# Weight requests, index products and the last tile's normalised rows between a hybrid block's mixer and its experts

## Chip, cores and metric

The kernel runs on one core of a Trainium2 chip. Its time is device microseconds (us) from start to end of the program on that core; a profiled execution also has a span, from the first to the last instruction of its trace. Five engines work side by side and wait for each other by semaphores: TensorE (PE; PEld is its weight load), VectorE (DVE), ScalarE (ACT), GpSimd (POOL) and SyncE (SP), which here issues nearly all DMA transfers from one queue.

## Reference

One decoder layer on 1024 tokens of 1024 channels, in float32. A mixer (a state space scan beside causal attention) is projected back to 1024 channels and added to the residual x. Then comes the part that matters here, a mixture of 32 experts in 4 groups:

```python
h = rms_norm(x, pre_norm_ffn) * (1.0 + sc2) + sh2
g_prob = softmax(h @ w_group_router + b_group)        # one group of 4
e_sel  = expert logits (8) of the chosen group
e_w, e_idx = top_k(softmax(e_sel), 2)                 # two experts of 8
hid = silu(h @ w_gate[e]) * (h @ w_up[e])             # 1024 -> 256
out = sum over the two experts of weight * (hid @ w_down[e])   # 256 -> 1024
x = x + g2 * rms_norm(out, post_norm_ffn)
```

Each expert has 3 MiB of weights: gate, up and down, 1 MiB each.

## The kernel before

The rows (tokens) are cut into NT = 8 tiles of P = 128. The trace of interest begins in the second half of the program, a loop over t from -3 to 7 that is written out for each engine. In step t the scan of tile t + 2 or t + 3, the output projection of tile t + 1 (`project`, L1523) and the routing of tile t (`h2_T_of` L1535, `route` L1542, `logits_of` L2004, `choose` L2007 to L2027) are interleaved by hand. For tile t the residual sum is `x2` (`x2_of`, L1981), the normalised row is `h2` = x2 * rstd * A2 + B2 (`h2_of` L1987 and `shifted` L1992, both on VectorE). SP stores both to DRAM (`x2_rows`, `h2_rows`) and loads the residual input of tile t + 2 (`load_x`, L1276). The profile prints names without buffer numbers, and so `x2` as `x`, `h2` as `h`.

*Slots.* Every token goes to two experts. Each expert's tokens are cut into halves of 64, and two halves, of the same expert or of neighbours, make one step of the expert stage (23 steps here). For that, the index stage counts tokens per expert (`both`, `before`: sums over a tile and over the tiles ahead; rank products with `tri_lt` and `ones`, L1590 and L1601 to L1604), gives each token a lane in its half (`own_rank`, `own_lane`, `lanes`) and a half (`half_j`), and turns these into a list of rows by matmuls of one-hot tables: `lane_v` (lane one-hot times token number, made by ScalarE at L1789 for tiles 0 to 6; `lane_last`, made by VectorE at L2053, for tile 7) against `half_oh` (L2138), at L1612. The lane table is written twice side by side, so that the 128 output rows hold the 64 lanes twice. Small VectorE instructions that need each other's results are chained by `link`, which waits for the one just issued. `busy(bank, n)` is n matmuls of `ident` by `ones` whose result nobody reads; they stand where TensorE would idle.

*Experts.* A gather on GpSimd (L1240) fetches the 128 rows of a step from `h2_rows`, TensorE turns them (L1621), multiplies by gate and up (L1645), turns the hidden layer, multiplies by down (L1671). The second half's weights are first copied to a common place by ScalarE and VectorE (`nearer`: L1826 and L2211). VectorE's L2205 evicts the result and so marks the end of a step. Weights live in a ring of RING = 6 slots that overlay buffers of earlier stages: slot 4 lies on the output projection's weights, slot 5 on `zs`, `h2`, the small scan tables and the router's weights. SP asks for the parts of experts 0 to 5 at hand-picked places, and from expert 6 on in the loop

```python
for e in range(RING, E):
    landed(e - 2)                      # all three parts of expert e-2
    used = last_step(e - RING)         # last step that reads expert e-6
    sp.wait_ge(S["gate_done"], used)
    load_gate(sp, e, r)
    sp.wait_ge(S["gu_done"], used)
    load_up(sp, e, r)
    sp.wait_ge(S["dn_done"], used)
    load_down(sp, e, r)
```

SP works through its list in order, so a wait holds back all that stands behind it, row stores as well.

## Time and profile before

| | |
|---|---|
| median of 3 runs | 1017.91 us (1013.28 to 1018.14) |
| profiled execution | 1020.63 us, of which its span is 1018.6 us |
| mean granted TensorE clock | 0.980 of full |
| TensorE busy | 963.5 us (95%) |
| VectorE busy | 514.3 us (50%) |
| ScalarE busy | 306.0 us (30%) |
| GpSimd busy | 215.5 us (21%) |
| moved by DMA | 192.56 MB, mean 189 GB/s |

All times of rows are microseconds from the span's start. The granted clock is a share of 2.4 GHz and has two levels, 1.00 and 0.50 (1.2 GHz); a mean between them is a stretch with both. A matmul in float32 appears as two passes, so counts of matmuls in rows are twice those in the code, except for transposes, which are one pass. The expert stage runs from about 690 to 973 us, the sums over the two experts and the output behind it to the end.

### The profile page before, as it was taken

How to read it: one execution, taken by the hardware profiler on the slowest of the kernel's cores; microseconds unless marked ns; L12 is line 12 of the kernel's file. 1: busy time of each engine (PE TensorE's matmuls, PEld its weight loads, DVE VectorE, ACT ScalarE, POOL GpSimd, SP SyncE). 2: the span in 40 equal slices, each digit the busy share in tenths (PEclk: the TensorE clock that was granted, in tenths of full speed). 3: DMA queues.
4: the chain of work that ended last, by engine and by line, in shares of the span. 5: the costliest groups of instructions: out<-in, count | busy, mean ns of one | idle time of the engine just before them, and what ended most of it. 6: DMA issues, size and time to landing. Idle time of an engine off the chain costs nothing.

```text
span 1018.6 us, 15260 instructions
## 1 busy us (share of the span) xinstructions
PE 963.5 (95%) x5501; PEld 578.7 (57%) x5501; DVE 514.3 (50%) x935; ACT 306.0 (30%) x598; POOL 215.5 (21%) x267
## 2 busy tenths in 40 slices
PE   8999999999989999989999999999999998999946
PEld 6544444444456556559666665695555554555512
DVE  2366456444765555556577775573333332333327
ACT  3220001223453434432232222133333332333313
POOL 2200001221600840003344322012222211222003
PEclk9999999999999999999999999999999998999968
DMA  9996523000000000005021121889999999999557
GB/s 323 359 357 227 190 82 52 0 1 0 7 1 1 1 2 1 1 1 208 1 83 62 63 83 62 350 317 361 420 416 407 398 396 391 418 405 407 201 218 289
DMA packets 54929, 192.56 MB, mean 189 GB/s; under 512 B 15354, under 2 KB 26690, under 8 KB 39362
## 3 DMA queue, kind: packets, MB, share of 16 engines
q1 hardware_dynamic: 46500, 173.10, 44.1%
q0 software_dynamic: 7056, 18.36, 4.7%
q8 instruction: 48, 0.79, 0.3%
q10 hardware_dynamic: 1296, 0.07, 0.1%
q14 instruction: 29, 0.24, 0.1%
HBM read 174.21 MB, written 24.64 MB: 195 GB/s over the span
## 4 chain that ended last, share of the span: by engine, by line
PE 36%; DMA 13%; DVE 2%; issue 1%; SPq 1%; ACT 1%; ACTq 0%; POOL 0%; POOLq 0%; DVEq 0%
PE PS L1523 11%; DMA ring<-in_w_down_dram 11%; PE PS L1645 8%; PE PS L1671 4%; PE PS L1437 1%; PE PS L1447 1%; PE PS L1701 1%; PE PS L1542 1%; PE PS L1491 1%; DMA ring<-in_w_gate_dram 1%; PE PS L1621 1%; PE PS L1535 1%; PE PS L1506 1%; DMA y_g<-y_rows 1%; DVE y_sum L2256 1%
## 5 line engine op out<-in xcount | busy, mean ns | idle before, releaser
L1645 PE MATMUL PS<-ring,xg_T 128*64 x736 | 165.5, 384 | 5.5 <-ACT near_gu L1826 4.5
L1645 PE MATMUL PS<-near_gu,xg_T 128*64 128x256 f32 x736 | 165.5, 384 | 0.0
L1645 PEld LDWEIGHTS PS<-ring,xg_T 128*64 128x64 f32 x736 | 101.8, 139 | 66.8 <-issue 21.0
L1523 PE MATMUL PS<-w_out_sb,cat_T 128*128 128x512 f32 x256 | 118.0, 603 | 1.4 <-DVE y_sc L1975 1.0
L1011 PE MATMUL PS<-hT,w_x 128*128 128x512 f32 x256 | 112.0, 594 | 0.0
L1645 PEld LDWEIGHTS PS<-near_gu,xg_T 128*64 128x64 f32 x736 | 101.8, 139 | 0.0
L434 POOL TENSOR_SCALAR rstd<-stat 128x1 f32<-128x1 f32 (+1 forms) x48 | 21.8, 453 | 372.4 <-ACT junk L614 181.3
L1671 PE MATMUL PS<-ring,hid_T 128*64 x184 | 83.8, 598 | 0.4 <-DVE hid_T L2198 0.4
L1671 PE MATMUL PS<-near_dn,hid_T 128*64 128x512 f32 x184 | 83.9, 598 | 0.0
L1011 PEld LDWEIGHTS PS<-hT,w_x 128*128 128x128 f32 x256 | 47.8, 190 | 58.1 <-issue 57.8
L915 DVE TENSOR_REDUCE row_max<-PS 128x1 f32<-128x1024 f32 (+7 forms) x64 | 48.2, 753 | 60.8 <-PE PS L1164 60.6
L2189 DVE TENSOR_TENSOR hid<-PS,hid_s 128x128 f32<-128x128 f32 x46 | 11.2, 286 | 129.2 <-PE PS L1645 129.2
L1162 PE MATMUL PS<-kT,qT 96*128 96x512 f32 (+4 forms) x192 | 74.9, 500 | 1.1 <-ACT qT L645 1.1
L661 ACT ACTIVATE probs<-PS,row_max 128x1024 f32<-128x1024 f32 (+7 forms) x64 | 47.4, 740 | 94.7 <-DVE row_max L915 94.3
L1523 PEld LDWEIGHTS PS<-w_out_sb,cat_T 128*128 128x128 f32 x256 | 47.0, 193 | 47.6 <-issue 47.3
L1240 POOL DMA_INDIRECT x_g<-h_rows,idx_i x23 | 39.8, 1729 | 152.3 <-PE PS L1621 135.3
L1060 PE MATMUL PS<-w_z,hT 128*128 128x512 f32 x128 | 56.2, 592 | 0.0
L1174 PE MATMUL PS<-ident,probs 128*128 128x128 f32 x288 | 43.4, 278 | 12.8 <-ACT probsT L669 6.6
L1174 PEld LDWEIGHTS PS<-ident,probs 128*128 128x128 f32 x288 | 30.9, 141 | 30.1 <-ACT probs L661 24.8
L1671 PEld LDWEIGHTS PS<-ring,hid_T 128*64 128x64 f32 x184 | 23.3, 136 | 42.6 <-issue 41.4
L1826 ACT ACTIVATE near_gu<-ring 128x2048 f32 x23 | 43.8, 1906 | 11.4 <-SPq L1306 7.8
L1069 PE MATMUL PS<-w_rest,hT 128*128 128x424 f32 x128 | 46.9, 519 | 0.0
(333 smaller groups left out, 1562.1 us busy)
## 6 DMA issues: line engine op xcount, KB each, us to landing
ring<-in_w_gate_dram SPq DMA_DIRECT2D x32, 1024.0 KB, 11.4
ring<-in_w_up_dram SPq DMA_DIRECT2D x32, 1024.0 KB, 13.4
ring<-in_w_down_dram SPq DMA_DIRECT2D x32, 1024.0 KB, 16.2
ada_later<-in_ada_w_dram SPq DMA_DIRECT2D x16, 1024.0 KB, 4.8
ada_first<-in_ada_w_dram SPq DMA_DIRECT2D x16, 512.0 KB, 9.6
y_g<-y_rows SPq DMA_DIRECT2D x8, 1024.0 KB, 11.9
x_in<-in_x_dram SPq DMA_DIRECT2D x8, 512.0 KB, 7.8
w_out_sb<-in_w_out_dram SPq DMA_DIRECT2D x1, 4096.0 KB, 13.1
```

Source lines behind the costliest of these rows:

```text
L661: act.activation(probs[b][:, 0:n], PS[:, 2 * b:2 * b + 2, :].rearrange("p a n -> p (a n)")[:, 0:n], ACT.Exp, bias=row_max[:, b:b + 1], acc ...
L915: dve.tensor_reduce(row_max[:, b:b + 1], PS[:, 2 * b:2 * b + 2, :].rearrange("p a n -> p (a n)")[:, 0:n], AX_X, ALU.max, negate=True).then ...
L1011: last = pe.matmul(BANK[4 + n % 4][:, :], w_x[:, k, ct * P:(ct + 1) * P], hT[:, k, hh * HALF:(hh + 1) * HALF], start=(k == 0), stop=(k == ...
L1060: last = pe.matmul(BANK[t % 2][:, 0:IN_SSD], hT[:, k, t * P:(t + 1) * P], w_z[:, k, :], start=(k == 0), stop=(k == KC - 1))
L1069: last = pe.matmul(BANK[6 + t % 2][:, 0:REST], hT[:, k, t * P:(t + 1) * P], w_rest[:, k, :], start=(k == 0), stop=(k == KC - 1))
L1162: pe.matmul(BANK[2 * b + c0 // HALF][:, 0:c1 - c0], qT[h][0:depth(h), i * P:(i + 1) * P], kT[h][0:depth(h), c0:c1], start=True, stop=c1 < ...
L1174: last = pe.transpose(BANK[4 + j // 4][:, j % 4 * P:(j % 4 + 1) * P], probs[g % 2][:, j * P:(j + 1) * P], ident[:, :])
L1240: pool.indirect_dma_start(x_g[n % 2][:, :], None, h2_rows, bass.IndirectOffsetOnAxis(ap=idx_i[:, n:n + 1], axis=0), bounds_check=T - 1, oo ...
L1523: last = pe.matmul(BANK[out_bank(t) + j], cat_T[t % 2][:, k, :], w_out_sb[:, k, j * HALF:(j + 1) * HALF], start=(k == 0), stop=(k == KC - 1))
L1645: last = pe.matmul(BANK[2 + s_][rows_, 0:FF], xg_T[b][:, k, rows_], gu[u][:, s_, k, :], start=(k == 0), stop=(k == KC - 1))
L1671: last = pe.matmul(BANK[5 + j][rows_, :], hid_T[b][:, k, rows_], (near_dn[k] if u else far[:, k, :])[:, j * HALF:(j + 1) * HALF], start=(k ...
L1826: act.activation(near_gu[:, 0, :], w[:, 0 * KC * FF:1 * KC * FF], ACT.Copy).then_inc(S["near_gu_act"], 1)
```

## The change

Weight requests are moved ahead on SP: expert 2, up and down of expert 3 and gate and up of expert 1 behind step t = 4 of the row loop; expert 0 and down of expert 1 in step 5; gate 3, expert 4 and gate 5 behind step 6; down 5 in step 7; up 5 stays behind the first gathers. Each stands behind waits for the last reader of what its space held. `lane_v` moves to a place that no slot uses.

The lane tables are written once, 64 wide, the index products give 64 rows, and VectorE reads them twice with a shift of partitions. For tile 7 alone, `h2` is made in another way: VectorE forms x2 * A2 and a diagonal matrix of rstd, TensorE adds the product of these to B2 in PSUM, and ScalarE copies the sum out. On VectorE the second lane comparison moves behind `choose`, and two chains of small instructions are interleaved, with waits (`after`) on marked ones. TensorE has fewer dummy matmuls; the rank products that need no result of tile 7 come first, and the counts get a semaphore of their own. `x2T_half` and a wait inside `route` split the router's transposes and products in halves, for each tile.

```diff
...
 lane_oh = place("lane_oh", R_S + 16384, [P, 2, NT, LANE])
-lane_v = place("lane_v", R_A + 137216, [P, 2, NT - 1, 2, LANE])
-lane_last = place("lane_last", R_A + 86016, [P, 2, 2, LANE])
+lane_v = place("lane_v", R_A + 24576, [P, 2, NT - 1, LANE])
+lane_last = place("lane_last", R_A + 86016, [P, 2, LANE])
+h2_diag = place("h2_diag", R_A + 86016 + 2 * LANE * 4, [P, P])
...
             if t == NT - 1:
-                sp.wait_ge(S["catT_done"], NT)
-                sp.wait_ge(S["yo_done"], NT - 1)
-                load_gate(sp, 3, 3)
+                sp.wait_ge(S["lg_done"], NT)
+                load_down(sp, 5, 5)
+            if t == NT - 3:
+                sp.wait_ge(S["ssd_y"], NT)
+                load_expert(sp, 0, 0)
+                sp.wait_ge(S["cat_done"], NT)
+                load_down(sp, 1, 1)
...
                 load_x(t + 2)
-            if t == NT - 3:
-                sp.wait_ge(S["ssd_y"], NT)
-                load_expert(sp, 0, 0)
-                sp.wait_ge(S["cat_done"], NT)
-                load_expert(sp, 1, 1)
+            if t == NT - 4:
+                sp.wait_ge(S["ssd_off"], NT - 1)
+                sp.wait_ge(S["ssd_m"], 2 * NT)
+                sp.wait_ge(S["cat_done"], 5)
                 load_expert(sp, 2, 2)
-        load_up(sp, 3, 3)
-        load_down(sp, 3, 3)
-        sp.wait_ge(S["yo_done"], NT)
-        load_gate(sp, 4, 4)
+                load_up(sp, 3, 3)
+                load_down(sp, 3, 3)
+                load_gate_up(sp, 1, 1)
+            if t == NT - 2:
+                sp.wait_ge(S["catT_done"], NT)
+                sp.wait_ge(S["yo_done"], NT - 1)
+                load_gate(sp, 3, 3)
+                sp.wait_ge(S["yo_done"], NT)
+                load_expert(sp, 4, 4)
+                sp.wait_ge(S["h2_stored0"], 16 * NT // 2)
+                load_gate(sp, 5, 5)
...
             return sp.value_load(free_i[0:1, e:e + 1], min_val=1, max_val=NTILE)
-        for e in range(RING - 3):
+        for e in range(RING - 2):
             landed(e)
-        sp.wait_ge(S["lg_done"], NT)
+        sp.wait_ge(S["h2_stored1"], 16 * NT // 2)
...
         sp.wait_ge(S["xg_loaded1"], 16)
-        load_up(sp, 4, 4)
-        load_down(sp, 4, 4)
-        load_expert(sp, 5, 5)
-        landed(RING - 3)
+        load_up(sp, 5, 5)
...
                 last = pe.transpose(BANK[4 + k // 4][:, k % 4 * P:(k % 4 + 1) * P], x2[t % 2][:, k::KC], ident[:, :])
+                if k == KC // 2 - 1:
+                    last.then_inc(S["x2T_half"], 1)
...
             pe.wait_ge(S["h2T_act"], t + 1)
-            pe.wait_ge(S["h2T_dve"], t + 1)
             for k in range(KC):
+                if k == KC // 2:
+                    pe.wait_ge(S["h2T_dve"], t + 1)
...
         pe.wait_ge(S["y_out"], NT - 1)
-        busy(7, 18)
+        for j in range(D // HALF):
+            pe.matmul(BANK[6 + j], ident[:, :], B2[:, j * HALF:(j + 1) * HALF], start=True, stop=False)
+        busy(3, 2)
         h2_T_of(NT - 1)
-        busy(7, 4)
         route(NT - 1)
-        busy(7, 16)
+        pe.wait_ge(S["h2_scaled"], 1)
+        for j in range(D // HALF):
+            last = pe.matmul(BANK[6 + j], h2_diag[:, :], y_sc[:, j * HALF:(j + 1) * HALF], start=False, stop=True)
+        last.then_inc(S["h2_sum"], 1)
+        busy(5, 2)
+        for b in (2, 3):
+            pe.matmul(BANK[b][:, 0:E], ones[:, :], before[:, NT - 1, :], start=True, stop=False)
         pe.wait_ge(S["rt_both"], NT)
-        pe.matmul(BANK[2][:, 0:E], ones[:, :], before[:, NT - 1, :], start=True, stop=False)
-        pe.matmul(BANK[2][:, 0:E], ones[:, :], both[:, NT - 1, :], start=False, stop=True)
-        pe.matmul(BANK[3][:, 0:E], tri_lt[:, :], both[:, NT - 1, :], start=True, stop=False)
-        pe.matmul(BANK[3][:, 0:E], ones[:, :], before[:, NT - 1, :], start=False, stop=True).then_inc(S["ranks_done"], 1)
-        busy(5, 22)
+        pe.matmul(BANK[2][:, 0:E], ones[:, :], both[:, NT - 1, :], start=False, stop=True).then_inc(S["counts_done"], 1)
+        pe.matmul(BANK[3][:, 0:E], tri_lt[:, :], both[:, NT - 1, :], start=False, stop=True).then_inc(S["ranks_done"], 1)
+        busy(5, 14)
+        pe.wait_ge(S["h2_done"], NT)
...
             for t in range(t0, t1):
-                rows_v = lane_last[:, j, :, :] if t == NT - 1 else lane_v[:, j, t, :, :]
-                last = pe.matmul(BANK[6][:, 0:2 * NTILE], rows_v.rearrange("p u n -> p (u n)"), half_oh[:, j, t, :],
+                last = pe.matmul(BANK[6][0:LANE, 0:2 * NTILE], lane_last[:, j, :] if t == NT - 1 else lane_v[:, j, t, :], half_oh[:, j, t, :],
...
         last.then_inc(S["idx_done"], 1)
-        busy(5, 26)
+        busy(5, 24)
...
         def h2T_half(t):
-            act.wait_ge(S["h2T_done"], t + 1)
+            act.wait_ge(S["x2T_half"], t + 1)
...
             for t in range(NT - 1):
-                last = act.activation(lane_v[:, j, t, :, :], lane_oh[:, j, t:t + 1, :].to_broadcast([P, 2, LANE]), ACT.Copy, scale=v_tab[:, j, t:t + 1])
+                last = act.activation(lane_v[:, j, t, :], lane_oh[:, j, t, :], ACT.Copy, scale=v_tab[:, j, t:t + 1])
             last.then_inc(S["lanes_scaled"], 1)
+            if j == 0:
+                act.wait_ge(S["h2_sum"], 1)
+                act.wait_ge(S["h2_stored1"], 16 * (NT // 2 - 1))
+                act.activation(h2[1][:, :], PS[:, 6:8, :].rearrange("p a n -> p (a n)"), ACT.Copy).then_inc(S["h2_done"], 1)
...
             for j in range(2):
-                ins = dve.tensor_scalar(lane_last[:, j, :, :], iota_row[:, 0:LANE].unsqueeze(1).to_broadcast([P, 2, LANE]),
-                                        lane[:, j, t:t + 1], v_tab[:, j, t:t + 1], ALU.is_equal, ALU.mult)
-            link(ins)
+                dve.tensor_scalar(lane_last[:, j, :], iota_row[:, 0:LANE], lane[:, j, t:t + 1], v_tab[:, j, t:t + 1], ALU.is_equal, ALU.mult)
...
                 h2T_half(t)
-                lanes(1)
...
                 choose(t)
-        h2_of(NT - 1)
+        def mark(ins):
+            step_dve[0] += 1
+            ins.then_inc(S["dve_step"], 1)
+            return step_dve[0]
+        def after(n):
+            dve.wait_ge(S["dve_step"], n)
+        dve.wait_ge(S["x2_done"], NT)
+        dve.tensor_tensor(y_sc[:, :], x2[(NT - 1) % 2][:, :], A2[:, :], ALU.mult)
+        dve.wait_ge(S["rstd_x2"], NT)
+        dve.tensor_scalar(h2_diag[:, :], ident[:, :], rstd[:, 6, NT - 1:NT], None, ALU.mult).then_inc(S["h2_scaled"], 1)
...
         wide = lambda v, n: v[:, :].unsqueeze(2).to_broadcast([P, NT, n])
-        shifted(NT - 1)
+        flat2 = lambda v: v[:, :, :].rearrange("p j t -> p (j t)")
+        lanes(1)
         dve.wait_ge(S["x2_stored0"], 16 * NT // 2)
-        dve.memset(near32, -FAR)
+        far_row = mark(dve.memset(near32, -FAR))
+        dve.wait_ge(S["counts_done"], 1)
+        halves = mark(dve.tensor_scalar(n_half, BANK[2][:, 0:E], 1.0, 1.0 / HT, ALU.max, ALU.mult))
         dve.wait_ge(S["ranks_done"], 1)
-        link(dve.tensor_scalar(n_half, BANK[2][:, 0:E], 1.0, 1.0 / HT, ALU.max, ALU.mult))
-        link(dve.tensor_scalar(n_half, n_half, 0.49, FAR, ALU.add, ALU.add))
-        link(dve.tensor_tensor_scan(incl, n_half, near32, 0.0, ALU.add, ALU.add))
-        link(dve.tensor_tensor(base_t, incl, n_half, ALU.subtract))
-        own_rank(NT - 1, NT, 3)
-        own_lane(NT - 1, NT)
+        for j in range(2):
+            hits = mark(dve.tensor_tensor(prod[:, j, NT - 1, :], picked[:, j, NT - 1, :], BANK[3][:, 0:E], ALU.mult))
+        after(halves)
+        whole = mark(dve.tensor_scalar(n_half, n_half, 0.49, FAR, ALU.add, ALU.add))
+        after(hits)
+        r, hi, lo = (v[:, :, NT - 1] for v in (rank, high, lane))
+        own = mark(dve.tensor_reduce(r, prod[:, :, NT - 1, :], AX_X, ALU.add))
+        after(whole)
+        summed_up = mark(dve.tensor_tensor_scan(incl, n_half, near32, 0.0, ALU.add, ALU.add))
+        after(own)
+        upper = mark(dve.tensor_scalar(hi, r, HT / 2 - 0.5, FAR * HT, ALU.subtract, ALU.add))
+        after(summed_up)
+        based = mark(dve.tensor_tensor(base_t, incl, n_half, ALU.subtract))
+        after(upper)
+        lower = mark(dve.scalar_tensor_tensor(lo, hi, FAR * HT, r, ALU.subtract, ALU.subtract, reverse1=True))
+        after(based)
+        of_base = mark(dve.tensor_tensor(prod[:, :, :, :].rearrange("p j t e -> p (j t) e"), picked[:, :, :, :].rearrange("p j t e -> p (j t) e"),
+                                         base_t.unsqueeze(1).to_broadcast([P, 2 * NT, E]), ALU.mult))
+        after(lower)
         last_lanes(NT - 1)
-        flat2 = lambda v: v[:, :, :].rearrange("p j t -> p (j t)")
-        link(dve.tensor_tensor(prod[:, :, :, :].rearrange("p j t e -> p (j t) e"), picked[:, :, :, :].rearrange("p j t e -> p (j t) e"),
-                               base_t.unsqueeze(1).to_broadcast([P, 2 * NT, E]), ALU.mult))
+        after(of_base)
...
         link(dve.scalar_tensor_tensor(flat2(half_j), flat2(high), 1.0 / HT, flat2(base_j), ALU.mult, ALU.add))
+        dve.wait_ge(S["h2_done"], NT)
...
         for u in range(2):
-            lanes_u = slice(u * LANE, (u + 1) * LANE)
-            ins = dve.tensor_scalar(put_f[lanes_u, :], BANK[6][lanes_u, u:2 * NTILE:2], ROUND - 1.0, None, ALU.add)
+            ins = dve.tensor_scalar(put_f[u * LANE:(u + 1) * LANE, :], BANK[6][0:LANE, u:2 * NTILE:2], ROUND - 1.0, None, ALU.add)
```

## Rows read from the trace of the kernel before

**Rows 1.** Chain of waits, in order of time: start, length, engine, line.
```profile
652.23 6.95 PE PS L1523 x16
...
677.41 3.79 PE PS L1612 x32
...
689.65 7.13 PE PS L1645 x64
...
701.78 6.91 PE PS L1645 x64
...
848.08 1.92 ACT near_gu L1826
850.23 9.86 PE PS L1645 x64
```

**Rows 2.** Timeline of VectorE, line 2205 alone: evictions that close steps.
```profile
701.83 0.69 DVE L2205 COPY y_e<-PS 128x512 f32<-128x512 f32 x1 [1.77 <-PE PS L1671]
713.75 0.69 DVE L2205 COPY y_e<-PS 128x512 f32<-128x512 f32 x1 [1.77 <-PE PS L1671]
...
809.59 0.69 DVE L2205 COPY y_e<-PS 128x512 f32<-128x512 f32 x1 [1.80 <-PE PS L1671]
...
834.51 0.69 DVE L2205 COPY y_e<-PS 128x512 f32<-128x512 f32 x1 [0.85 <-PE PS L1671]
...
865.21 0.69 DVE L2205 COPY y_e<-PS 128x512 f32<-128x512 f32 x1 [1.79 <-PE PS L1671]
...
973.03 0.69 DVE L2205 COPY y_e<-PS 128x512 f32<-128x512 f32 x1 [3.45 <-PE PS L1671]
```

**Rows 3.** Stretches: busy time of five engines, granted clock, DMA share, GB/s.
```profile
624.00:626.00 2.00, 2.00 (x3) 0.68 (x2) 0.82 (x2) 0.20 (x1) 1.77 (x1) 0.50 0.26 109
677.00:681.00 4.00, 4.00 (x36) 3.82 (x35) 1.02 (x3) 0.00 (x0) 0.00 (x0) 1.00 1.01 422
850.00:854.00 4.00, 3.77 (x18) 2.25 (x20) 1.82 (x2) 0.60 (x1) 0.00 (x0) 0.50 1.00 418
```

**Rows 4.** Timeline of SP's queue: when weight parts are asked for.
```profile
639.69 0.43 SPq L1213 DMA_DIRECT2D ring<-in_w_gate_dram  x1
...
689.64 0.33 SPq L1217 DMA_DIRECT2D ring<-in_w_up_dram  x1
...
713.74 0.33 SPq L1221 DMA_DIRECT2D ring<-in_w_down_dram  x1
716.98 0.33 SPq L1213 DMA_DIRECT2D ring<-in_w_gate_dram  x1
...
835.86 0.33 SPq L1213 DMA_DIRECT2D ring<-in_w_gate_dram  x1
```

**Rows 5.** Timeline: a residual tile asked for, and the last residual sum.
```profile
618.09 0.33 SPq L1276 DMA_DIRECT2D x<-in_x_dram  x1
...
662.70 1.22 DVE L1981 TENSOR_TENSOR x<-y_sc,x 128x1024 f32<-128x1024 f32 x1
```

**Rows 6.** Instructions of line 1217, requests of up parts (1 MiB each).
```profile
DMA to landing us min/median/max: 4.9/13.4/15.2
```

**Rows 7.** Timeline of the index stage.
```profile
670.58 0.19 DVE L2023 TENSOR_TENSOR both<-picked 128x32 f32<-128x32 f32 x1
...
672.46 0.19 DVE L2125 TENSOR_SCALAR late<-PS 128x32 f32<-128x32 f32 x1 [0.51 <-PE PS L1604]
...
674.37 0.60 DVE L2053 TENSOR_SCALAR lane_last<-iota_row,rank,v_tab 128x128 f32<-128x128 f32 x2
...
676.66 1.36 DVE L2138 TENSOR_TENSOR half_oh<-iota_row,base_j 128x512 f32<-128x512 f32 x3
...
682.80 1.19 POOL L1240 DMA_INDIRECT x_g<-h_rows,idx_i  x1 [16.74 <-DVE idx_i L2148]
```

**Rows 8.** Weight loads of TensorE by shape: count, busy us, mean ns, idle before.
```profile
L1187 PEld LDWEIGHTS PS<-probsT,v_sb 128*64 128x64 f32 x576 | 30.8, 136 | 5.6 <-issue 4.5 <-DVE probsT L922 0.6
...
L1612 PEld LDWEIGHTS PS<-half_oh,lane_v 128*128 128x128 f32 x28 | 3.3, 192 | 0.2 <-DVE half_oh L2138 0.2
```

More of the change, by code:

```diff
@@ L308, in hybrid_block @@
             rstd_y rstd_yo rstd_x2 rank_early rev_made gate_done u_loaded0 u_loaded1 u_loaded2 u_loaded3 u_loaded4 u_loaded5
-            d_loaded0 d_loaded1 d_loaded2 d_loaded3 d_loaded4 d_loaded5 u_ready d_ready u_here d_here router_exp route_act ranks_done slots_done idx_done idx_read dst_read lanes_made lanes_scaled""".split()
+            d_loaded0 d_loaded1 d_loaded2 d_loaded3 d_loaded4 d_loaded5 u_ready d_ready u_here d_here router_exp route_act ranks_done slots_done idx_done idx_read dst_read lanes_made lanes_scaled x2T_half counts_done h2_scaled h2_sum""".split()
         EARLY = """x_loaded0 x_loaded1 win_x_loaded0 win_rest_loaded ada_loaded0 ada_loaded1 first_loaded2 ada_row_loaded
```

## The prediction, made before the changed kernel was run

> **What bounds the kernel now.** I read the page first. TensorE is busy nearly throughout, which says little, since the kernel fills its gaps with dummy matmuls. So I went to the chain of waits [rows 1]. From 652 us on it shows two places that this change touches. One is the index stage, from the end of the last output projection (652.23 + 6.95 = 659.2) to the first expert product at 689.65, which I call T0: 30.5 us in which the last row tile is routed and every token gets a slot. The other stands in the middle of the expert stage: at 848.08 ScalarE copies weights, and TensorE starts only when this is done (850.23).
>
> The evictions that close each step [rows 2] size the second place. Steps 2 to 10 take (809.59 - 701.83)/9 = 11.97 us each, steps 15 to 23 take (973.03 - 865.21)/9 = 11.98. Steps 11 and 12 together take 24.92, steps 13 and 14 30.70. Over 22 steps the loss is 271.20 - 22 x 11.98 = 7.6 us. Of these, 1.0 is in steps 11 and 12, and 6.7 in 13 and 14. There the gate and up product takes 9.86 and not 6.91, 2.95 more [rows 1]: the granted clock was 0.50 of full from 850 to 854 [rows 3], that is 1.2 GHz, after TensorE had idled for the other 3.8.
>
> Why the weights are late: expert e may be asked for when SP has seen expert e-2 land and expert e-6 is used up. From expert 8 (716.98) to 21 (835.86) the gate parts are asked for every 118.88/13 = 9.14 us [rows 4], and each request follows a landing: these are paced by the transfers. TensorE wants an expert every 23 x 11.98/32 = 8.6 us on average, faster where experts have few tokens. So the lead of the first six experts is eaten up until step 14.
>
> **Weights.** Before, the first part is asked for at 639.69 and the up part of expert 4 only at 689.64 [rows 4]; from the one to the other come 13 MiB. After the change, the block at t = 4 stands behind the residual load that is issued at 618.09 [rows 5]; its semaphores (state products, masks, fifth concatenation) belong to work already past by then, so I count no wait. One MiB costs 2.5 us at the 422 GB/s of a full stretch [rows 3]; one alone landed in 4.9 [rows 6], so 2.4 is start-up. In the queue up to the last residual tile lie 0.5 + 7 + 0.5 + 4 + 0.5 + 0.5 = 13 MiB: landed by 618.1 + 2.4 + 32.5 = 653. That tile is read at 662.70 [rows 5], so 10 us are to spare, and behind SP's new waits stands only this row traffic. Two MiB more (rows, gate 3) are done by 658. At 659.2 the projection frees expert 4's slot: 3 MiB, gate 5, the last residual rows, down 5 and the last normalised rows make 6 MiB, landed by 659.2 + 2.4 + 15 = 676.6. So at T0 all but up 5 are there.
>
> What is this worth? Not the 4 MiB of lead in full: the ring is then full, and later parts wait for TensorE. Down 7 is asked for at 713.74 = T0 + 24.1, at the end of step 2, before and after alike [rows 2, 4]. Gate 8 then follows at T0 + 24.9 with only down 7 ahead of it, so it lands at about T0 + 24.9 + 4.9 + 2.5 = T0 + 32. Before, it was asked for at T0 + 27.3 and, taking the 12.2 us of gate 21 from 835.86 to the copy at 848.08 [rows 1, 4], landed at T0 + 39.5. With 9.14 us an expert from there, gate 21 lands at T0 + 151 in place of T0 + 158.4. Step 14 would start without delay at T0 + 155.7, and the copy takes 1.9 + 0.2 ahead of it, so the part is wanted by T0 + 153.5. It is there with 2.5 to spare; steps 11 to 13 have more. So the whole 7.6 goes, the half clock with it. Bounds: 0 (a pace 6% slower, 9.72) to 7.6. Where the stall goes, nothing is late next: the steps at 11.98 before and after it show what TensorE alone takes.
>
> **Index stage.** Three savings on one chain.
> First, the counts. The last choice of experts is ready at 670.58 + 0.19 = 670.8, but VectorE starts on the counts at 672.46 [rows 7]: dummy matmuls, and rank products that don't need that choice, stand ahead on TensorE. After the change those products come early, two are left of which the count is first, and VectorE has a lane comparison (some 0.6, moved behind the choice) and a memset to get through: 671.4, 1.05 sooner. Bounds 0 to 1.1.
> Second, VectorE's chain from 672.46 to the slot comparison at 676.66, 4.2 us. Nine small instructions take 1.91 (to 674.37), each waiting out the one before, then the lane comparison of the last tile 0.60 [rows 7]: 2.5 ahead of the wide product. Woven as two chains they are some four pairs of 0.25, 1.05; the lane comparison is half as wide and moves behind the wide product, 0.25. The 1.65 of wide product, sum and last step stay. I get 2.9, a saving of 1.3; bounds 0.3 (only the narrower lane comparison) to 1.5.
> Third, the index products: 32 passes in 3.79 [rows 1], 0.118 each. A pass moves 64 columns and loads 128 columns of weights; loads of 128 take 192 ns, of 64 take 136 [rows 8], 56 less. So a pass of 64 by 64 takes some 0.06. The products still wait for the third comparison, which ends 1.36 after the first starts [rows 7]: they end some 2.7 after that start, not 4.53 (677.41 + 3.79 - 676.66): 1.8 less. No row has such a pass alone; bounds 0 to 1.85, and I stand near the upper one since the load is what the rows show as longest.
> Sum 4.2 us, bounds 0.3 to 4.5. Gather, weight copies and T0 all follow the index, so T0 moves by as much.
>
> What is added is hidden. Four passes of B2 stand in dummies' place; four of the scaled rows (0.43 each, 6.95/16 in [rows 1]) run from 667.9 to 669.6 while VectorE chooses until 670.8. With dummies and older products they leave 0.3 us; beyond that the ranks slip one for one. ScalarE's copy of the result, taken at the 1.22 of VectorE's row of that width [rows 5], is done by 670.8; VectorE's slot comparison, which overwrites its input, wants it at 674.3. ScalarE's second seven lane scalings follow it, some 2 us before their products. The split wait of the router gives nothing: ScalarE has its square to finish first. With no cover these additions would cost 2 us.
>
> **Sum.** 1018.6 - 7.6 - 4.2 = 1006.8 of span; the profiled execution took 1020.63, so 1008.8 beside it. That execution lies 2.7 above the median of the runs (1017.91), and I forecast from the median: 1006.1.
>
> **Rivals.**
> *The clock falls in the index stage* (0.20). It stood at 0.50 from 624 to 626 [rows 3] after nothing but narrow matmuls, the diagonal products and the router's. The change leaves TensorE idle for some 2 us where dummies ran (662 until the residual sum at 662.70 + 1.22, [rows 5]), with narrow router matmuls right behind, and makes the index products narrow. Against it: dummies stay later on, and no idle stretch is as long as the 3.8 ahead of 850. At half clock the scaled rows, dummies and older products take 2.6 us more, 2.3 beyond their cover; with index or token products slow too, up to 4 are lost: 1008.5 to 1010. The Trainium skill (TensorE: Matmul & The Clock Gate, Part 1) speaks for this rival: it calls the throttled state the default, which only activity releases. By that rule the dummies taken out cost the index gain, 1010; the trace agrees with it around 850.
> *The stall stays in part* (0.14). At 9.5 us an expert gate 21 lands at T0 + 155.5, 2 late; at 9.7, 4.6 late, and the half clock comes back: 1008 to 1013.
> *Hidden anyway* (0.06). The gather also waits for the last normalised rows, stored behind down 5. I have them landed at 676.6, and the gather's start moved from 682.80 [rows 7] to 678.6. If they land 6 us later the index gain is gone; with the stall kept as well, 1013 to 1018. The Trainium skill (DMA: Bandwidth & Descriptors, Queues, rings and completion order) says that a DMA engine takes one queue's descriptors in ring order. By it these rows wait for all 5.5 MiB ahead, which is how I counted; no row here shows it.
> *Slower* (0.04). The last residual tile, now behind 12.5 MiB, comes after 662.70. Each us late is one of the whole; it outweighs 11.8 from 674.5 on, where the queue would move 245 GB/s. At 220 GB/s it lands at 682: 1025. The full stretch in [rows 3] speaks against it.
>
> **Numbers.** Forecast 0.56, its own range 1003 to 1009. The range 1001.5 to 1012.5 takes in both index bounds, a stall kept in part, and at the low end the lowest run of before (1013.28) less 11.8. Some 0.5%, 5 us, is what can be told from no change. Faster by more: forecast, clock and half of the stall rival, 0.83; within, 0.12; slower, 0.05.
>
> **What the profile would show.** Weight parts asked for from about 618.5; first expert product near 685.4; index passes 0.06 apart; steps 11.98 apart through 11 to 14; granted clock 1.00 from 660 to 690. Wrong if a step still waits on a weight copy, if the clock shows 0.50 ahead of T0, or if the gather starts on the row store and not on the index.

## The result and the profile after

| | before | after |
|---|---|---|
| median | 1018.00 us (15 runs, 1013.28 to 1022.14) | 1012.54 us (15 runs, 1009.51 to 1017.72) |
| profiled execution / span | 1020.63 / 1018.6 us | 1012.54 / 1010.8 us |
| first rank product / T0 | 659.02 / 689.65 | 659.00 / 689.33 |
| evictions of step 1 to step 23 | 271.20 us | 264.31 us |
| last eviction to the span's end | 45.6 us | 45.0 us |

The ratio of the times is 0.9947, with a 95% interval of [0.9933, 0.9961]: 5.4 us less. The changed kernel is faster, by a little less than half of what I forecast (11.8). In the profiled executions the table says at once where a part is missing: the expert stage gave 6.9 of 7.6 us, and T0 moved by 0.3 in place of 4.2.

The index stage comes first. Here is the table of stretches of the kernel after, with the columns of [rows 3]:

```profile
662.00:664.00 2.00, 0.12 (x2) 0.04 (x1) 1.96 (x3) 0.06 (x1) 0.00 (x0) 1.00 1.01 426
664.00:666.00 2.00, 1.50 (x12) 1.30 (x12) 1.64 (x4) 2.00 (x6) 0.74 (x2) 1.00 1.00 422
666.00:668.00 2.00, 2.00 (x16) 2.00 (x15) 1.18 (x2) 1.24 (x6) 0.05 (x1) 0.72 1.02 430
668.00:676.00 8.00, 8.00 (x27) 5.93 (x28) 5.04 (x27) 2.69 (x8) 0.00 (x0) 0.50 0.97 367
676.00:678.00 2.00, 2.00 (x15) 2.00 (x15) 1.93 (x6) 0.00 (x0) 0.00 (x0) 0.72 0.38 156
678.00:680.00 2.00, 2.00 (x29) 1.88 (x28) 0.43 (x2) 0.00 (x0) 0.00 (x0) 1.00 0.02 6
```

The first number behind the length is TensorE's busy time: 0.12 of 2 us from 662 to 664. The granted clock, third from the end, then falls to 0.50, and is back at 1.00 only from 678 on. What this does to the work shows in the timeline of TensorE, same stretch:

```profile
663.96 1.16 PE L1543 MATMUL PS<-ident,x 128*128 128x128 f32 x8 [1.88 <-DVE x L2001]
665.63 2.52 PE L1553 MATMUL PS<-w_r,h_T 128*128 128x36 f32 x16 [0.50 <-ACT h_T L1779]
667.96 3.76 PE L1612 MATMUL PS<-y_sc,h_diag 128*128 128x512 f32 x4
...
673.08 0.61 PE L1619 MATMUL PS<-both,ones 128*128 128x32 f32 x2
673.50 0.61 PE L1620 MATMUL PS<-both,tri_lt 128*128 128x32 f32 x2
673.93 4.88 PE L1445 MATMUL PS<-ones,ident 128*128 128x128 f32 x28
678.74 1.03 PE L1628 MATMUL PS<-half_oh,lane_v 128*64 128x64 f32 x14
```

TensorE waits 1.88 us for the residual sum where 18 dummies stood before, and 0.50 more ahead of the router (L1553). The four passes of scaled rows (L1612) take 3.76 where I counted 1.7, and the 28 passes of dummies that I took for cover (L1445) run to 678.74 and hold back the index products, whose input VectorE began to write at 677.07. That is the answer to [rows 7] in VectorE's timeline:

```profile
673.73 0.19 DVE L2156 TENSOR_SCALAR late<-PS 128x32 f32<-128x32 f32 x1 [2.19 <-PE PS L1619]
...
677.07 1.36 DVE L2183 TENSOR_TENSOR half_oh<-iota_row,base_j 128x512 f32<-128x512 f32 x3
...
681.27 0.18 DVE L2192 TENSOR_SCALAR idx_i<-put_f 128x32 int32<-128x32 int32 x1
```

VectorE waits 2.19 us for the counts, which come at 673.73, not at 671.4 as forecast (2.3 late). The chain to the slot comparison takes 3.34, not 2.9 (0.4), and the products end 1.05 later than 2.7 behind the comparison. Together these three, 3.8, are nearly all of the 3.9 us that T0 lacks.

In the expert stage the evictions of step 1, 2, 10 to 14 and 23 answer to [rows 2] (timeline of VectorE):

```profile
701.51 0.69 DVE L2249 COPY y_e<-PS 128x512 f32<-128x512 f32 x1 [1.77 <-PE PS L1687]
713.43 0.69 DVE L2249 COPY y_e<-PS 128x512 f32<-128x512 f32 x1 [1.77 <-PE PS L1687]
...
809.26 0.69 DVE L2249 COPY y_e<-PS 128x512 f32<-128x512 f32 x1 [1.80 <-PE PS L1687]
821.24 0.69 DVE L2249 COPY y_e<-PS 128x512 f32<-128x512 f32 x1 [1.63 <-PE PS L1687]
833.22 0.69 DVE L2249 COPY y_e<-PS 128x512 f32<-128x512 f32 x1 [1.80 <-PE PS L1687]
847.31 0.68 DVE L2249 COPY y_e<-PS 128x512 f32<-128x512 f32 x1
858.01 0.69 DVE L2249 COPY y_e<-PS 128x512 f32<-128x512 f32 x1 [1.80 <-PE PS L1687]
...
965.82 0.69 DVE L2249 COPY y_e<-PS 128x512 f32<-128x512 f32 x1 [3.45 <-PE PS L1687]
```

All steps take 11.98, but for 13 and 14 with 24.79 together: 0.8 too much, where 7.6 were lost before. The chain of waits still shows one wait on weights there, in the place of the one in [rows 1]:

```profile
831.22 12.24 DMA ring<-in_w_gate_dram
843.61 1.92 ACT near_gu L1846
845.77 7.13 PE PS L1661 x64
```

The gate part of expert 21, asked for at 831.22, lands 12.24 later, ScalarE copies it, and step 14 starts at 845.77. It now runs at full clock: 7.13, where it took 9.86.

### The profile page after: what moved, and what is told of

It is laid out like the page before. It is cut to its first block, busy times and chain, and to the rows that moved or that the text cites. A ratio compares the mean times of both kernels' runs of the same rounds, so it can differ in the third digit from the quotient of the medians.

```text
span 1010.8 us, 15099 instructions
## 1 busy us (share of the span) xinstructions
PE 956.8 (95%) x5421; PEld 571.0 (56%) x5421; DVE 512.7 (51%) x935; ACT 305.7 (30%) x599; POOL 216.6 (21%) x267
## 4 chain that ended last, share of the span: by engine, by line
PE 47%; DVE 3%; DMA 2%; issue 1%; ACT 1%; ACTq 0%; POOL 0%; SPq 0%; POOLq 0%; DVEq 0%
PE PS L1661 15%; PE PS L1531 11%; PE PS L1687 8%; PE PS L1637 2%; PE PS L1455 1%; PE PS L1717 1%; PE PS L1553 1%; DMA ring<-in_w_gate_dram 1%; PE PS L1499 1%; PE PS L1670 1%; PE PS L1514 1%; DMA y_g<-y_rows 1%; PE PS L1445 1%; PE PS L1543 1%; DVE y_sum L2305 1%
## 5 line engine op out<-in xcount | busy, mean ns | idle before, releaser
L1661 PE MATMUL PS<-ring,xg_T 128*64 x736 | 162.7, 379 | 1.6 <-ACT xg_T L1821 1.0
L1661 PE MATMUL PS<-near_gu,xg_T 128*64 128x256 f32 x736 | 162.7, 379 | 0.0
```

The lines of the kernel that those rows point to most:

```text
L1661: last = pe.matmul(BANK[2 + s_][rows_, 0:FF], xg_T[b][:, k, rows_], gu[u][:, s_, k, :], start=(k == 0), stop=(k == KC - 1))
```

## The experiments

All kernels ran beside the kernel before, the kernel after in a group of its own and the others in four. A ratio is that of the times of all runs (5 to 15 of the kernel) to those of the kernel before in the same group, with its 95% interval; where a text below gives a time "by the ratio", it is worked out from this. Two numbers of each profiled execution size the two terms: from the first rank product to T0 (30.63 before, 30.33 after), and what the 22 steps behind the first lose against 22 x 11.98 = 263.56 (7.6 before). "Clock" is the stretch ahead of T0. Each kernel has one profiled execution.

| kernel | ratio to before | to T0 | clock | steps lose |
|---|---|---|---|---|
| after | 0.9947 [0.9933, 0.9961] | 30.33 | 0.50 for 10 us | 0.8 |
| weights_only | 0.9957 [0.9938, 0.9976] | 30.60 | 1.00 | 0.2 |
| index_only | 0.9981 [0.9965, 0.9998] | 30.15 | 0.50 for 10 us | 7.5 |
| after_fill | 0.9935 [0.9914, 0.9956] | 27.28 | 1.00 | 1.0 |
| after_wide | 0.9968 [0.9946, 0.9990] | 32.91 | 0.50 for 14 us | 1.7 |
| before_thin | 1.0025 [1.0006, 1.0045] | 35.00 | 0.50 for 10 us | 4.2 |
| fill_first_gap | 0.9920 [0.9901, 0.9940] | 26.88 | 1.00 | 4.7 |
| index_fill | 0.9958 [0.9940, 0.9975] | 27.44 | 1.00 to 686 | 4.7 |
| fill_rows_first | 0.9917 [0.9897, 0.9937] | 26.47 | 1.00 | 1.8 |
| before_light | 0.9936 [0.9921, 0.9951] | 30.57 | 1.00 | none |
| after_light | 0.9933 [0.9916, 0.9949] | 31.27 | 0.50 for 14 us | none |
| first_gap_rows | 0.9922 [0.9894, 0.9949] | 26.26 | 1.00 | 2.8 |
| fill_second_gap | 0.9953 [0.9936, 0.9971] | 31.67 | 0.50 for 14 us | 0.5 |
| first_gap_rows_light | 0.9894 [0.9860, 0.9928] | 26.52 | 1.00 | none |

### The two halves apart

`weights_only` is the kernel before with SP's list of the kernel after, `index_only` the kernel after with SP's list of before.

The first, from before (the rest of SP's list is that of the diff ahead of the prediction):

```diff
-lane_v = place("lane_v", R_A + 137216, [P, 2, NT - 1, 2, LANE])
+lane_v = place("lane_v", R_A + 24576, [P, 2, NT - 1, 2, LANE])
...
+                    if t == NT - 4:
+                        sp.wait_ge(S["ssd_off"], NT - 1)
+                        sp.wait_ge(S["ssd_m"], 2 * NT)
+                        sp.wait_ge(S["cat_done"], 5)
+                        load_expert(sp, 2, 2)
...
```

The second, from after:

```diff
...
-                        load_down(sp, 1, 1)
...
-                    if t == NT - 4:
-                        sp.wait_ge(S["ssd_off"], NT - 1)
-                        sp.wait_ge(S["ssd_m"], 2 * NT)
-                        sp.wait_ge(S["cat_done"], 5)
+                        load_expert(sp, 1, 1)
                         load_expert(sp, 2, 2)
-                        load_up(sp, 3, 3)
...
```

> The kernel before with the new weight requests alone (lane tables only moved out of slot 5's space). If the weights alone bring what the change brings: steps 11 to 14 take 48 to 49 us together (55.6 before, 48.7 after), T0 stays at 689.6 +- 0.3, and the time is 6 to 8 us below before, ratio 0.992 to 0.994. Rival (the stall goes only because the index stage changed too, or the early requests delay the row stores): steps 11 to 14 above 52 us, or T0 later than 691, and the ratio within 0.997 to 1.003.

> The changed kernel with the weight requests of before. If the index part is worth what the changed kernel's trace shows (T0 0.3 us sooner, 10 us at half clock): T0 689.2 to 689.8, steps 11 to 14 55 to 56 us as before, ratio 0.998 to 1.001. Rival (the index part gains and something of the weight traffic takes it back, the stores behind 5.5 MiB for instance): T0 685 to 687 and a ratio of 0.995 to 0.997.

The early requests alone take the steps' loss from 7.6 to 0.2 us and leave the index stage as it was (30.60); the index part alone leaves the loss (7.5) and moves T0 by 0.5, at half clock. So in these traces neither term moves the other's stage, the expert stage's gain is all the requests', and the index part's is missing without them too. By the ratio the requests give 4.4 us [2.4, 6.3], less than the 6 to 8 that I had expected and than the 7.4 of the profiled execution, and the index part gives 1.9 [0.2, 3.6]. The profiled execution of `weights_only`, 1008.64, is the fastest of its 12 (median 1013.67).

### The clock and the idle stretches

`after_fill` fills both idle stretches of TensorE with dummies; `fill_first_gap` has the first edit of its diff alone (the long stretch, ahead of the transposes), `fill_second_gap` the second alone.

```diff
-        busy(3, 2)
+        busy(3, 10)
         h2_T_of(NT - 1)
+        busy(3, 2)
         route(NT - 1)
```

`before_thin` takes dummies out of the kernel before.

```diff
-        busy(7, 18)
+        busy(7, 10)
         h2_T_of(NT - 1)
-        busy(7, 4)
         route(NT - 1)
```

> The changed kernel with 8 more dummy matmuls ahead of the last tile's transposes and 2 behind them. Clock theory (the index gain is lost because TensorE idles from 662 to 664 and the clock falls to half from 666.9 to 677): the granted clock stays 1.00 up to T0, counts on VectorE at 671.4 to 672.0, T0 at 685 to 686.5, time 3 to 4 us below the changed kernel, ratio to before 0.989 to 0.992. Work theory (the four passes of the scaled rows and the new waits cost the gain at any clock): clock 1.00, but T0 no sooner than 688.5 and the time within 1 us of the changed kernel.

> The kernel before with fewer dummy matmuls around the last tile's transposes: 10 in place of 18 ahead of them, none in place of 4 behind them; nothing else is changed. Clock theory: what drops the clock in the changed kernel is the idle time of TensorE there (2 us ahead of the transposes, half a us behind them), whoever leaves it. Then this kernel shows a granted clock of 0.50 for 7 to 10 us from about 8 us after the first rank product, its remaining dummies run at half rate and hold back the counts, the first eviction comes 45 to 47 us after the first rank product (42.8 before), and the time is 2 to 4 us above that of before. Rival: the diagonal product of the scaled rows or the narrower index products drop the clock, and the idle time alone does not. Then the clock stays 1.00 from the first rank product to the first expert product, the stage stays at 42.8 and the time is that of before.

> The changed kernel with the first of its two idle stretches filled (10 dummies in place of 2 ahead of the last tile's transposes); the half us ahead of the last router products stays idle. Theory that the long stretch decides: clock 1.00 through the index stage, first eviction 39.5 us after the first rank product, as with both stretches filled, time near 1010. Rival that the short stretch and the narrow products behind it are enough: a granted clock of 0.50 for several us from the router products on, first eviction 41 to 42.5 us after the first rank product, time 1012 to 1013.

> The changed kernel with only the second, short idle stretch filled (two dummies ahead of the last router products); the 2 us ahead of the transposes stay idle. Theory that the long stretch decides: half clock for 7 to 10 us as in the changed kernel, first eviction 42.3 to 43 us after the first rank product, time 1012 to 1013. Rival that one filled stretch of either kind is enough: clock 1.00, first eviction 39.1 to 39.5 us after the first rank product, time 1010 to 1010.6.

With both stretches filled the clock stays at 1.00, and T0 comes 3.3 us sooner than before in place of 0.3. By the ratio `after_fill` takes 6.6 us [4.5, 8.8] less than before, not the 8 to 11 that I had expected. The long stretch alone decides: with it filled the clock holds through the half us ahead of the router (26.88); with only the short one filled it falls, for 14 us and not for the expected 7 to 10 (31.67, longer than before). All six traces of kernels with the long stretch filled show 1.00 from the first rank product to T0 or, in `index_fill`, to 686; all six with it idle show the fall. In five of these six, all but `after`, it came right behind the idle stretch of 1.8 to 1.9 us, before the transposes there had ended, ahead of the router's and the diagonal products. So it does not need them. In `index_only`, TensorE's timeline has

```profile
661.49 1.84 PE L1536 MATMUL PS<-ident,x 128*128 128x128 f32 x8 [1.88 <-DVE x L1994]
```

where the same transposes take 1.16 at full clock. And in the kernel before, which has neither the diagonal product of the rows nor narrow index products, the clock falls as well when its dummies are thinned: T0 comes 4.4 us later, and by the ratio it takes 2.5 us [0.6, 4.6] more. Its stretches:

```profile
663.00:665.00 2.00, 0.51 (x5) 0.32 (x3) 1.97 (x2) 0.00 (x0) 0.00 (x0) 1.00 1.09 410
665.00:675.00 10.00, 8.80 (x41) 8.43 (x42) 6.63 (x21) 5.83 (x17) 0.79 (x2) 0.54 0.79 310
675.00:677.00 2.00, 2.00 (x16) 2.00 (x16) 0.53 (x2) 0.00 (x0) 0.00 (x0) 0.76 0.35 141
```

Again a stretch of 0.51 busy of 2 us stands ahead of the fall. So the removed dummies are the cause of the fall, not what the change added.

### The index term at full clock, and the products alone

`after_wide` has the index products 128 rows wide again, their tables written twice (`lane_last` too, and VectorE reads the halves in place). `index_fill` is `index_only` with the two edits of `after_fill`.

```diff
 after_wide
-lane_v = place("lane_v", R_A + 24576, [P, 2, NT - 1, LANE])
+lane_v = place("lane_v", R_A + 24576, [P, 2, NT - 1, 2, LANE])
...
-                last = act.activation(lane_v[:, j, t, :], lane_oh[:, j, t, :], ACT.Copy, scale=v_tab[:, j, t:t + 1])
+                last = act.activation(lane_v[:, j, t, :, :], lane_oh[:, j, t:t + 1, :].to_broadcast([P, 2, LANE]), ACT.Copy, scale=v_tab[:, j, t:t + 1])
...
```

> The changed kernel with the lane tables written twice, 128 columns of weights to an index product as before. If a pass of 64 by 64 is limited by its weight load: index passes 0.118 apart here and 0.063 in the changed kernel, 3.8 us in place of 2.1 for the 32, T0 1.5 to 1.9 us later than the changed kernel's 689.3, time 1 to 2 us above it. Rival (the products are limited by the comparisons on VectorE or by the wait on dummies): T0 less than 0.7 us later.

> The changed kernel with the weight requests where they were before, and with both idle stretches of the index stage filled with dummies. Theory that my index term of 4.2 us was right and only lost to the clock: first eviction 38.5 to 39.2 us after the first rank product (42.8 before, 42.3 without the dummies), the steps 11 to 14 still lose 7 to 8 us, time 3.5 to 4.5 us below that of before. Rival that the term was too large, the clock being a side matter: first eviction 40.5 to 42 us after the first rank product at a clock of 1.00, time 1 to 2 us below that of before.

In `after_wide` the products take, by TensorE's timeline,

```profile
679.34 1.67 PE L1628 MATMUL PS<-half_oh,lane_v 128*128 128x64 f32 x14
680.85 0.39 PE L1628 MATMUL PS<-half_oh,lane_last 128*128 128x64 f32 x2
681.07 1.73 PE L1628 MATMUL PS<-half_oh,lane_v 128*128 128x64 f32 x14
682.63 0.39 PE L1628 MATMUL PS<-half_oh,lane_last 128*128 128x64 f32 x2
```

3.68 us, against 2.02 for the 32 passes of the kernel after (678.81 in its chain of waits): 0.115 and 0.063 a pass. Only these 1.7 us of the 2.6 by which its T0 is later are the width's; its half clock also lasted longer. Behind T0 its clock fell a second time (0.50 from 692 to 694), and the first step took 1.6 us more than in the kernel after.

`index_fill` lacks the early requests; the last step of its index (`idx_i` on VectorE) starts 18.33 us behind the first rank product (22.63 before), 4.3 sooner, but T0 comes only 3.2 sooner. By the ratio it takes 4.3 us [2.5, 6.1] less; its steps lost 4.7 in the profiled execution, not the 7 to 8 expected. There the stretches show where 1 us went, and a second fall of the clock:

```profile
682.00:686.00 4.00, 2.08 (x17) 1.70 (x15) 1.83 (x2) 3.27 (x3) 0.00 (x0) 1.00 0.50 169
686.00:692.00 6.00, 5.07 (x24) 2.91 (x26) 0.69 (x1) 1.47 (x2) 0.99 (x1) 0.50 0.78 296
```

The dummies behind the index products end before the gathered rows are there, which land 5.9 us behind the gather's start (4.8 before) beside weights in flight. TensorE idles 1.9 us, the clock falls, and the first expert step runs slow: the first eviction comes 42.5 us after the first rank product (42.8 before). I had expected 38.5 to 39.2, so this run does not show the index term whole.

### The gather and the row store

In `after_fill` the gather starts 1.65 us behind the start of `idx_i` (1.15 before), and the profile names the landing of `h_rows` as what it waited for. `fill_rows_first` is `after_fill` with SP's last two items exchanged; `first_gap_rows` is the same with the first stretch alone filled.

```diff
-                    if t == NT - 1:
-                        sp.wait_ge(S["lg_done"], NT)
-                        load_down(sp, 5, 5)
...
                     sp.dma_start(h2_rows[t * P:(t + 1) * P, :], h2[t % 2][:, :]).then_inc(S[f"h2_stored{t % 2}"], 16)
+                    if t == NT - 1:
+                        sp.wait_ge(S["lg_done"], NT)
+                        load_down(sp, 5, 5)
```

> The changed kernel with both idle stretches filled, and with the store of the last normalised rows ahead of the down part of expert 5 in SP's list instead of behind it. Theory that the gather there waited for the landing of these rows behind the weights: with the down part behind them it starts 1.1 to 1.2 us after the index (1.65 with the weights ahead), the first eviction comes 0.5 to 1.0 us sooner (38.5 to 39.0 us after the first rank product), nothing waits for the down part, time near 1009.5. Rival that the gather is late by the load of the DMA engines and not by the order in the queue: its start and the first eviction stay where they were (39.5), time near 1010.

> The changed kernel with only the first idle stretch filled, and the store of the last normalised rows ahead of the down part of expert 5. Theory that both gains add: first eviction 38.1 to 38.5 us after the first rank product (39.07 with the one, 38.65 with the other beside two more dummies), clock 1.00 in the index stage, time 1009 to 1010. Rival that what the row store gives is taken back: 39.0 or more, time 1010.5.

GpSimd's timeline in `after_fill` and in `fill_rows_first`:

```profile
677.07 1.19 POOL L1241 DMA_INDIRECT x_g<-h_rows,idx_i  x1 [12.93 <-DMA h_rows<-h]
...
677.23 1.19 POOL L1241 DMA_INDIRECT x_g<-h_rows,idx_i  x1 [12.44 <-DVE idx_i L2193]
```

The gather starts 1.15 behind `idx_i` in `fill_rows_first` and `first_gap_rows`, and T0 comes 0.8 sooner than in `after_fill` (26.47) and 1.0 sooner (26.26). Of this 0.5 is the wait; the rest lies behind the gather's start, where its rows took 5.2 us to land in `after_fill` and 4.9 and 4.7 in the two others. `first_gap_rows` has the shortest index stage of all, 4.4 us less than before. TensorE there, by stretches:

```profile
660.00:662.00 2.00, 2.00 (x18) 1.81 (x17) 1.97 (x3) 0.00 (x0) 0.00 (x0) 1.00 0.99 410
662.00:664.00 2.00, 1.40 (x11) 1.21 (x11) 1.63 (x6) 1.92 (x5) 0.60 (x2) 1.00 1.04 442
664.00:672.00 8.00, 7.75 (x58) 6.68 (x58) 7.13 (x31) 4.18 (x14) 0.18 (x1) 1.00 0.98 373
```

Its median is 1008.04 (6 runs, 1006.55 to 1015.4); by the ratio it takes 7.9 us [5.2, 10.8] less than before, where the kernel after gave 5.4. The four kernels with the early requests and the long stretch filled (0.9917 to 0.9935) can't be told apart by their intervals. Each of them gains more than each of the three whose clock falls (`after`, `after_wide`, `fill_second_gap`: 0.9947 to 0.9968), but the intervals of the two sets overlap: that filling pays beside the kernel after is likely, not settled by the runs.

### What the stall is worth, and whether two leftovers are all

`before_light` and `after_light` load half of each down part from expert 6 on; `first_gap_rows_light` is `first_gap_rows` with that edit.

```diff
-                    load_down(sp, e, r)
+                    sp.dma_start(w_dn[r][:, 0, :], wd_v[e][:, 0, :]).then_inc(S[f"d_loaded{r}"], 16)
```

> The kernel before, but from expert 6 on only the first half of each down part is loaded (2.5 MiB an expert in place of 3); the other half keeps an older expert's numbers. TensorE's work is unchanged. Theory: the stall of the expert stage is the transfers' pace and nothing else, and it differs between executions (7.6 us in the profiled one, 4.7 in that of the index part with filled stretches). Then steps 2 to 23 take 263.6 to 264.0 us, no half clock around 850, and the median falls by 4 to 6 us, to 1012.5 to 1014. By my prediction, which put the whole stall of one execution into the median, it falls by 7.6, to 1010.5. Rival: the stall has another cause (the copies on ScalarE, the clock by itself): the steps keep 268 us or more.

> The changed kernel with the same halved down parts from expert 6 on. Theory: the early requests leave a small stall, of 0.2 to 4.7 us by the execution, since the ring is full until the first experts are used up and the transfers' pace decides again from expert 9 on. Then the steps 2 to 23 take 263.6 to 264.0 us and the median is 0.5 to 2.5 us below that of the changed kernel (1012.5), 1010 to 1012. Rival: nothing of the stall is left in the median of the changed kernel, and the time stays at 1012 to 1013.

> The kernel of the filled first stretch with the row store ahead of the down part, and with the halved down parts from expert 6 on. Theory that the clock in the index stage and the rest of the stall are all that the changed kernel misses of my sum: clock 1.00 from the first rank product to the first expert product, first eviction 38.1 to 38.6 us after the first rank product, steps 2 to 23 in 263.5 to 264.0 us, and 10 to 11.5 us less than before (a ratio of 0.9887 to 0.9902), near the sum of the halved parts alone (6.5) and the index part with filled stretches alone (4.3). Rival that the two overlap or that something else gives the time back: 8 to 9 us less than before, as with the full down parts (0.9917 to 0.9922), though the stages are as short as named.

The stall comes from the transfers: `before_light` loses nothing in its steps, its evictions of steps 1 and 23 in VectorE's timeline being

```profile
698.73 0.69 DVE L2205 COPY y_e<-PS 128x512 f32<-128x512 f32 x1 [1.77 <-PE PS L1671]
...
962.21 0.69 DVE L2205 COPY y_e<-PS 128x512 f32<-128x512 f32 x1 [3.45 <-PE PS L1671]
```

263.48 apart. With the requests of before and full parts, four profiled executions lost 7.6, 7.5, 4.7 and 4.2 us, so one execution did not size this term. The clock is part of the spread: around 850 it stood at 0.50 for some 7 us in the traces of before and `index_only`, for 3.4 in `index_fill` (4.7 lost) and not at all in `before_thin` (4.2). By the ratio the whole stall is worth 6.5 us [5.0, 8.0], above my 4 to 6 by its middle, with the predicted 7.6 inside the interval. `after_light` stands at 0.9933 where after stands at 0.9947, some 1.4 us less, with overlapping intervals: what is left of the stall there is small and not sized any better. With the clock held, the rows stored first and the halved parts, the time falls by 10.8 us [7.3, 14.3], and in the profiled execution the two stages are 4.1 and 7.7 us shorter than before, 11.8 together. The rival's 8 to 9 us lie inside the interval; the stages speak against it. These kernels leave out half of the down weights, so they size a limit and are no better kernels.

## Why the prediction was partly right and partly wrong

The forecast of 1006.1 lies 6.4 below the median after. In spans, profiled against profiled, it is 4.0: the index stage 3.9 and the stall 0.7, with 0.6 won at the tail. The other 2.4 are the step from the profiled execution to the median: I took off 2.7 because the execution before lay above its median, and the one after lies at its median (with 0.3 less around its span). By the runs both terms fall short: the requests gave 4.4 us [2.4, 6.3] where I had 7.6, the index part 1.9 [0.2, 3.6] where I had 4.2.

**Weights: the mechanism was right, its price was that of one execution.** Parts are asked for from 620.21 (forecast 618.5), the last residual tile is not late (its sum at 662.68, [rows 5] has 662.70), and in the profiled execution 6.9 of 7.6 us are gone. But 7.6 was the loss of one execution. The four traces with the requests of before lose 6.0 on average, the eight with the early requests and full parts 1.7: 4.3 apart, as the runs of `weights_only` say (4.4). One step inside was off as well. I had gate 21 landed at T0 + 151, with 2.5 us to spare; it landed at T0 + 154.1, and the steps lost 0.8. I had let the lead of 7.4 us live on from gate 8, counting that part alone. But its neighbours wait for TensorE as well while the ring is full, as SP's timeline shows:

```profile
714.66 0.33 SPq L1214 DMA_DIRECT2D ring<-in_w_gate_dram  x1
...
721.61 0.33 SPq L1214 DMA_DIRECT2D ring<-in_w_gate_dram  x1
...
731.09 0.33 SPq L1214 DMA_DIRECT2D ring<-in_w_gate_dram  x1
732.31 0.33 SPq L1218 DMA_DIRECT2D ring<-in_w_up_dram  x1
737.38 0.33 SPq L1222 DMA_DIRECT2D ring<-in_w_down_dram  x1
```

Gate 8 is asked for at T0 + 25.3 (forecast 24.9), but down 10 only at 737.38, with the eviction of step 4. The stretches behind T0, with the DMA share next to last:

```profile
694.00:704.00 10.00, 10.00 (x76) 5.67 (x74) 4.10 (x8) 3.94 (x4) 2.52 (x2) 1.00 0.82 283
704.00:714.00 10.00, 10.00 (x76) 5.62 (x74) 3.38 (x7) 3.35 (x5) 2.44 (x2) 1.00 0.92 318
714.00:724.00 10.00, 10.00 (x82) 6.01 (x79) 3.52 (x8) 3.76 (x5) 2.49 (x2) 1.00 0.96 349
```

In the same stretches of before the share is 1.02, 1.01 and 1.02. By the differences, 3.5 us of transfer are not used (an estimate). From gate 9 on the pace is (831.22 - 721.61)/12 = 9.13, as before. So gate 21 was asked for 4.3 us sooner against T0 (141.9 for 146.2), not 7.4.

That leaves no reserve, and the rival *The stall stays in part* comes true in a small way, more in one execution than in another: the pace of the requests from gate 9 to 21 was 9.17 in `weights_only` (0.2 lost), 9.24 in `after_wide` (1.7) and 9.34 in `fill_first_gap` (4.7, some at half clock).

**Index stage: the clock was wrong.** Here the prediction failed. The step was *What is added is hidden*: the scaled rows at 0.43 a pass, and dummies and older products as cover with 0.3 us left, are all counted at the durations of full clock. The runs show 0.50 there for 10 us, 3.76 for the four passes, and T0 sooner by 0.3 us in place of 4.2. I had named the rival, *The clock falls in the index stage*, with its place and cause, and gave it 0.20, because dummies stay later on and no idle stretch was as long as the 3.8 us ahead of 850. It is what happened, though the stretch was 1.9 us long. I had 2.3 us for the rows, dummies and older products, and up to 4 in all; the runs show 3.9. What I missed in price is that dummies, doubled in length, stop being cover: 28 passes of them, most at half clock, held TensorE until 1.7 us behind the start of the slot comparison, where before the dummies ended 0.75 behind it.

At full clock the sum of the three savings comes out, as VectorE's timeline of `first_gap_rows` shows:

```profile
668.35 0.19 DVE L2043 TENSOR_TENSOR both<-picked 128x32 f32<-128x32 f32 x1
...
669.04 0.19 DVE L2156 TENSOR_SCALAR late<-PS 128x32 f32<-128x32 f32 x1
...
672.18 1.36 DVE L2183 TENSOR_TENSOR half_oh<-iota_row,base_j 128x512 f32<-128x512 f32 x3
...
675.47 0.18 DVE L2192 TENSOR_SCALAR idx_i<-put_f 128x32 int32<-128x32 int32 x1
```

The counts are read 11.90 us behind the first rank product (669.04 - 657.14) against 13.44 before: 1.54, where I had 1.05 and a bound of 1.1. The choice of experts is itself ready 0.35 sooner (11.21 for 11.56), which I had put at nothing. VectorE's chain takes 3.14 against 4.20: 1.06 for 1.3. The index follows the comparison by 3.29 against 4.99: 1.70 for 1.8, at 0.06 a pass. That is 4.3 us, for 4.2; that the sum fits so well is luck, since the first term was too small and the other two too large.

The rule of the Trainium skill (TensorE: Matmul & The Clock Gate, Part 1) that I set beside this rival, that half rate is the resting state and activity lifts it, agrees with `before_thin`: there nothing but activity was taken away, and the clock fell to 0.50. I should have given the rival more for a reason that the trace showed: before 624 the clock fell to 0.50 with only 0.3 us idle on TensorE, right behind diagonal and router products that had run at 1.00, and the output projection of 624 to 626 [rows 3] ran at 0.50. No run separates what brought that fall; `weights_only` has the same work there and kept 1.00.

**The gather: right for the kernel after, a small wait behind it.** In the kernel after it starts 1.15 behind the index, as before. In `after_fill`, whose index is faster, the rival *Hidden anyway* holds for 0.5 us: the last rows are asked for behind the down part of expert 5 and land late. The Trainium skill (DMA: Bandwidth & Descriptors, Queues, rings and completion order) has a DMA engine take one queue's descriptors in ring order; the trace of `fill_rows_first`, where only the order of the two items is changed, agrees, by these 0.5 us.

**The slower rival** did not show: SP's early blocks hold nothing back, and up to the first rank product the profiled executions before and after agree within 0.02 us.

What stays open is how much the steps of the kernel after lose in its other executions: the profiled one is at the median and loses 0.8, but only one of each kernel has a trace.

## What to carry to other kernels

A dummy that stands in a gap is part of the price of what follows it: before taking any out, look in the stretches for what TensorE does right behind the gap, and give the fall of the clock the chance that the kernel's other gaps suggest, with dummies and cover doubled in length. Asking for weights sooner helps for as long as the ring is not yet full. Once it is full, requests wait for TensorE and transfer time goes unused, so count the last part of each expert and not its first. Size a stall from several executions, not from the one that was profiled. A stage's gain is best tested with the other stage's limit taken away, as halved transfers did here.

## What the runs showed of the hardware

The clock falls on less than I thought: TensorE idle for 1.88 us, with 1.16 us of transposes, 0.50 idle and narrow router products behind it, was followed by 0.50 for 10 us in the kernel after, and the same idle stretch by 14 us in `fill_second_gap`, through long runs of full-width dummies. With 10 dummies in the gap there was none, although 0.5 us stayed idle. But no length of the idle stretch alone tells whether the clock falls: `after_fill` idled 1.75 us ahead of its first gathered rows, and `before_thin` 2.85 of the 4 us from 852 to 856, both at 1.00 and with no fall behind them.

Executions also differ by where else the clock falls. The trace of before has 0.50 around 460 and 626, that of `before_light`, the same program up to expert 6, nowhere before the tail, and its first rank product came 3.0 us sooner (655.98). Over the 12 executions of `weights_only` the time goes with the mean granted clock, from 1008.64 us at 0.991 to 1018.68 at 0.980. So the some 10 us at half clock in the row loop of before go with 3 us there, as much as an edit of the index stage is worth, and the times of few runs carry this.

A float32 pass of 64 columns with 64 columns of weights takes 0.063 us, one with 128 columns of weights 0.115 to 0.118. The weight loads of [rows 8] are longer for 128 columns too (192 and 136 ns); that they set this pace is not shown.
